# Blocks of 32 instead of 16 in a triangular inverse: the solve in three parts between other work, one join level fewer, units prepared a query group sooner

## The chip, the cores and the metric

The kernel runs on one core of a Trainium2 chip. The metric is the device time in microseconds of one execution. One program computes two networks, one behind the other: a first block (stages mix0, mlp0, mix1, mlp1; 512 tokens, model width 1024) and a second block of two layers (layer0, layer1; 16 meta tokens ahead of the 512, so 528). The change touches only the two layers of the second block, each in the same way.

## What is computed

Each layer of the second block adds a mixer and a gated feed-forward part. The mixer has two branches and gates on them: sparse attention (4 heads, keys chosen by an indexer) and a gated DeltaNet (4 heads of 128), whose chunks of tokens need the solution of a unit lower triangular system:

```python
m = jnp.where(strict, bc[..., None] * kk * decay, 0.0)
lhs = m + jnp.eye(CHUNK, dtype=f32)
rhs = jnp.concatenate([vc * bc[..., None], kc * (bc * jnp.exp(gcum))[..., None]], axis=-1)
sol = lax.linalg.triangular_solve(lhs, rhs, left_side=True, lower=True, unit_diagonal=True)
u, w = sol[..., :A_DV], sol[..., A_DV:]
...
v_new = u_c - jnp.einsum('bhcd,bhde->bhce', w_c, S)
o = (jnp.einsum('bhcd,bhde->bhce', q_c * jnp.exp(g_c)[..., None], S)
     + jnp.einsum('bhcs,bhse->bhce', qk_c, v_new))
S = (S * jnp.exp(g_last)[..., None, None]
     + jnp.einsum('bhcd,bhce->bhde', k_c * jnp.exp(g_last[..., None] - g_c)[..., None], v_new))
```

`S` goes from chunk to chunk, so the chunks run one behind the other. Everything is float32.

## The kernel before

**Weights.** All weights are streamed from HBM in 436 pieces of 128x1024. SyncE loads a piece, ScalarE rounds it to `w_hi` (L1314), GpSimd makes the remainder `w_lo` (L631, four instructions a piece), and TensorE multiplies in three passes (`n_hi,w_hi`, `n_lo,w_hi`, `n_hi,w_lo`).

**Filling.** In the attention and DeltaNet stages of a layer TensorE has a hand-set order. The small matmuls of the stage stand between pieces of projection work that depends on nothing in the stage, the fillers (the output gate `z`, the branch gates). `fill(blocks)` issues that many blocks of the current piece; a block is six matmuls (L1068), a piece is eight blocks. A piece adds up in one pair of PSUM banks, so the next piece waits until VectorE has evicted the last one (semaphore `taken`; evictions L2464, L2576). The tables `SCORE_FILL`, `VALUE_FILL` (attention) and `FILL` (the slots below) say how many blocks stand where.

**Attention.** `attention()` runs over four query groups j = 0 to 3 of 128 queries. A group first has its score phase: for each of four heads TensorE makes the scores (L1241, L1246), VectorE shifts them (L2848, L2851, with a row reduction), ScalarE exponentiates them (L1924), VectorE normalises them (L2862, L2863). VectorE takes a head's normalisation after the next head's shift. Then the value phase: transposes (L1272), copies on ScalarE (L1943), products with the values (L1280).

**Units.** The 528 tokens are five units: unit 0 with the 16 meta tokens, units 1 to 4 with 128 each. The matrices of a unit are prepared inside the attention (`prepare_keys` and `prepare_queries` on TensorE, `prepare` on VectorE with `unit_staged` as its output), and ScalarE sends them to an array `unit_scratch` in HBM. `NEXT_UNIT` and `EARLY` say in which query group.

**Inverse.** The inverse of `lhs` is built in two steps. The diagonal blocks of 16x16 of all units are read back from the scratch array, one block to a partition and two sets (128 partitions x 2 x 256 elements), and inverted on VectorE by substitution (`solve_blocks`): 15 steps of one multiplication (L2746) and one subtraction (L2749), then a transposing copy (L2750). `send_solved` writes the inverses X and their transposes Y back with ScalarE's DMAs, in rows of 64 bytes. Then the unit is read as whole 128x128 matrices of four heads (`fetch_unit`: M, X, Y). TensorE and VectorE join neighbouring blocks at the levels 4, 5 and 6, from 16 to 32, 64 and 128: `join_half` (4 matmuls), a copy on ScalarE (`p`, L1845), `join` (8 matmuls, or 4 at the last level, where only Y is needed), and subtractions on VectorE (L2795, L2796 by `joined_both`; L2838). Unit 0 has a single 16x16 block and needs no join.

**Slots.** Behind the attention come slots s = 0 to 5. Slot s joins unit s (s = 1 to 4), makes its `w` and `u` (`w_and_u`) and takes unit s - 1 through the recurrence (`step_v`, `step_state`, `step_out`). In `tokens` (L1104, L1105) keys and values are turned to rows of tokens; `v_tok` (L1860) are ScalarE's copies of the latter. In all loops the queue of each engine is in order, so an instruction that waits holds up all behind it on its engine.

## Time and profile before

| | |
|---|---|
| median of 3 runs | 2883.15 us (2881.82 to 2883.48) |
| the profiled execution | 2884.77 us |
| its span, first to last instruction | 2882.9 us |
| mean granted TensorE clock | 0.994 |
| TensorE busy | 2831.2 us, 98% of the span |
| VectorE, ScalarE, GpSimd busy | 51%, 35%, 48% |

The span lies in the profiled execution's time; 1.9 us of that lie around it. Layer 0 has its attention and slots from about 1300 to 1530 us of the span, layer 1 some 891 us later with the same pattern. A row of a timeline begins with start and duration in us; what stands in brackets at its end is how long the engine was idle before it, and who ended that. "ACTq" is ScalarE issuing a DMA. The clock is a share of 2.4 GHz.

### The profile page before, as it was taken

How to read it: one execution, taken by the hardware profiler on the slowest of the kernel's cores; microseconds unless marked ns; L12 is line 12 of the kernel's file. 1: busy time of each engine (PE TensorE's matmuls, PEld its weight loads, DVE VectorE, ACT ScalarE, POOL GpSimd, SP SyncE). 2: the span in 40 equal slices, each digit the busy share in tenths (PEclk: the TensorE clock that was granted, in tenths of full speed). 3: DMA queues.
4: the chain of work that ended last, by engine and by line, in shares of the span. 5: the costliest groups of instructions: out<-in, count | busy, mean ns of one | idle time of the engine just before them, and what ended most of it. 6: DMA issues, size and time to landing. Idle time of an engine off the chain costs nothing.

```text
span 2882.9 us, 43826 instructions
## 1 busy us (share of the span) xinstructions
PE 2831.2 (98%) x17572; PEld 2496.0 (87%) x17572; DVE 1463.4 (51%) x2401; ACT 1000.5 (35%) x1494; POOL 1374.4 (48%) x1748
## 2 busy tenths in 40 slices
PE   9999999999999999999999999999999999999999
PEld 7768888877788888998899999999988799999887
DVE  8955322267532227896445544234797545444241
ACT  4453222255322224433443322223443434322221
POOL 6416554555655455542125555456552214555554
PEclk9989999999999999999999999999999999999999
DMA  5103333322333334222414233223322423333322
GB/s 186 59 22 103 101 95 89 102 95 73 96 101 89 95 102 125 97 76 87 112 56 144 85 93 92 88 90 94 111 79 64 123 69 105 106 100 91 96 95 73
DMA packets 124622, 271.09 MB, mean 94 GB/s; under 512 B 22808, under 2 KB 59032, under 8 KB 124184
## 3 DMA queue, kind: packets, MB, share of 16 engines
q1 hardware_dynamic: 73104, 246.05, 27.1%
q10 hardware_dynamic: 51336, 22.41, 2.9%
q8 instruction: 139, 2.28, 0.3%
q14 instruction: 43, 0.35, 0.0%
HBM read 250.35 MB, written 18.07 MB: 93 GB/s over the span
## 4 chain that ended last, share of the span: by engine, by line
PE 86%; DVE 10%; issue 1%; ACT 1%; ACTq 1%; POOL 0%; DMA 0%; DVEq 0%; POOLq 0%
PE acc L659 65%; PE acc L1068 5%; PE aux L1082 3%; PE acc L708 3%; DVE index_score L2686 2%; PE acc L1049 2%; PE aux L1049 2%; DVE best L2682 2%; PE acc L692 1%; DVE conv_out L2101 1%; PE acc L1082 1%; PE aux L959 1%; PE acc L1280 1%; PE acc L782 1%; PE aux L846 0%
## 5 line engine op out<-in xcount | busy, mean ns | idle before, releaser
L631 POOL TENSOR_TENSOR w_lo<-w_raw,w_hi 128x256 fp32r<-128x256 f32 x1744 | 1374.2, 820 | 1492.3 <-ACT w_hi L1314 1491.6
L659 PE MATMUL acc<-n_hi,w_hi 128*128 128x264 f32 (+1 forms) x2824 | 757.1, 323 | 2.3 <-DVE index_k L2387 1.3
L659 PE MATMUL acc<-n_lo,w_hi 128*128 128x264 f32 (+1 forms) x2824 | 748.1, 320 | 0.0
L659 PE MATMUL acc<-n_hi,w_lo 128*128 128x264 f32 (+1 forms) x2824 | 746.0, 319 | 0.0
L1314 ACT ACTIVATE w_hi<-w_raw 128x1024 fp32r<-128x1024 f32 (+1 forms) x436 | 454.4, 1044 | 628.9 <-PE acc L659 560.9
L659 PEld LDWEIGHTS acc<-n_hi,w_hi 128*128 128x128 f32 x2824 | 470.4, 188 | 60.7 <-issue 15.9
L659 PEld LDWEIGHTS acc<-n_lo,w_hi 128*128 128x128 f32 x2824 | 467.2, 188 | 40.9 <-issue 2.6
L659 PEld LDWEIGHTS acc<-n_hi,w_lo 128*128 128x128 f32 x2824 | 467.2, 188 | 38.3
L2203 DVE TENSOR_TENSOR x<-x,acc 128x512 f32<-128x512 f32 (+1 forms) x144 | 99.7, 692 | 565.6 <-PE acc L659 519.2
L659 PE MATMUL acc<-hidden_lo,w_hi 128*128 128x512 f32 (+1 forms) x1040 | 343.3, 358 | 0.0
L659 PE MATMUL acc<-hidden_hi,w_lo 128*128 128x512 f32 (+1 forms) x1040 | 342.7, 357 | 0.0
L659 PE MATMUL acc<-hidden_hi,w_hi 128*128 128x512 f32 (+1 forms) x1040 | 342.7, 357 | 0.0
L659 PEld LDWEIGHTS acc<-hidden_lo,w_hi 128*128 128x128 f32 x1040 | 183.8, 188 | 31.0
L659 PEld LDWEIGHTS acc<-hidden_hi,w_hi 128*128 128x128 f32 x1040 | 183.5, 188 | 31.0
L659 PEld LDWEIGHTS acc<-hidden_hi,w_lo 128*128 128x128 f32 x1040 | 184.1, 188 | 30.0
L2364 DVE SCALAR_TENSOR_TENSOR unit_a<-acc,norm_scale 128x512 f32<-128x512 f32 x64 | 44.3, 692 | 196.3 <-PE acc L659 196.1
L1599 ACT ACTIVATE hidden_hi<-unit_b 128x512 fp32r<-128x512 f32 x64 | 40.5, 632 | 260.4 <-DVE unit_b L2369 260.4
L1068 PE MATMUL acc<-n_hi,w_hi 128*128 128x264 f32 x480 | 120.0, 332 | 6.4 <-DVE x L2464 2.7
L1770 ACT ACTIVATE squares<-unit_b 128x528 f32<-128x528 f32 x44 | 28.4, 646 | 261.8 <-DVE unit_b L2652 261.8
L2641 DVE TENSOR_TENSOR unit_a<-acc,norm_scale 128x528 f32<-128x528 f32 x44 | 31.1, 708 | 167.2 <-PE acc L659 167.1
L1068 PE MATMUL acc<-n_lo,w_hi 128*128 128x264 f32 x480 | 98.6, 287 | 0.0
L1068 PE MATMUL acc<-n_hi,w_lo 128*128 128x264 f32 x480 | 98.5, 287 | 0.0
(490 smaller groups left out, 3781.8 us busy)
## 6 DMA issues: line engine op xcount, KB each, us to landing
w_raw<-in_stream SPq DMA_DIRECT2D x420, 512.0 KB, 3.5
unit_blocks<-unit_scratch ACTq DMA_DIRECT2D x30, 256.0 KB, 4.9
w_raw<-in_stream SPq DMA_DIRECT2D x16, 384.0 KB, 3.0
unit_scratch<-unit_staged ACTq DMA_DIRECT2D x20, 256.0 KB, 2.6
saved_x<-x SPq DMA_DIRECT2D x2, 2112.0 KB, 9.4
x<-saved_x SPq DMA_DIRECT2D x16, 264.0 KB, 2.7
saved_gates<-root ACTq DMA_DIRECT2D x12, 264.0 KB, 2.1
unit_scratch<-unit_staged ACTq DMA_DIRECT2D x1, 2560.0 KB, 12.9
```

Of the source, the lines that this page charges most:

```text
L631: i = pool.tensor_tensor(wl[:, slot, s], raw[:, slot, s], wh[:, slot, s].bitcast(F32), ALU.subtract)
L659: last = pe.matmul(o, w[:, p % W_SLOTS, P * b:P * b + P], r, start=(b == 0 and i == 0), stop=(b == n - 1 and i == 2))
L708: mm = pe.matmul(acc[:, bank_of(p), :], w[:, p % W_SLOTS, P * b:P * b + P], v[b], start=(n == 0 and i == 0), stop=(n == KT - 1 and i == 2))
L1049: mm = pe.matmul(banks[:, 2 * g + s, 0:HALF], w[:, p % W_SLOTS, P * b:P * b + P], v[:, b, HALF * s:HALF * s + HALF], start=(b == 4 * g and ...
L1068: mm = pe.matmul(acc[:, s, 0:HALF], w[:, p % W_SLOTS, P * b:P * b + P], v[:, b, HALF * s:HALF * s + HALF], start=(b == 0 and i == 0), stop ...
L1082: return pe.matmul(out, lhs, rhs, start=start, stop=stop)
L1314: act.activation(wh[:, q % W_SLOTS, 0:n], raw[:, q % RAW_SLOTS, 0:n], ACT.Copy)\
L1599: act.activation(hid_hi[:, q % 2, m, ROW], sb_[:, m % 2, 0:SEQ], ACT.Copy)\
L2203: dve.tensor_tensor(xm, xm, a, ALU.add).then_inc(taken, c.made(taken))
L2364: dve.scalar_tensor_tensor(u, a, 0.0, scale[:, ROW], ALU.max, ALU.mult)\
L2682: latest[j] = step(dve.max(best[:, j - 1, :], s))
L2686: latest[j] = step(dve.match_replace(s, best[:, j - 1, :], s, MARK))
```

## The change

- **Blocks.** `SMALL` goes from 16 to 32, `LEVELS` from (4, 5, 6) to (5, 6). A joined unit has two `join_half` and two joins, of which the last is the short one. Gone for each joined unit are one `join_half` and one full join: 12 matmuls of 128x128, their ScalarE copy and two VectorE subtractions.
- **The solve.** 68 blocks (4 units x 4 heads x 4, and the 4 of unit 0) lie on 68 partitions, and the substitution has 31 steps, 62 instructions. Step j works on (31 - j)(j + 1) elements of a partition: 31 at both ends, 256 in the middle. It is in parts: the start and steps 0 to 9 behind the normalisation of query group 2; steps 10 to 15 inside the score phase of group 3, two behind the shift of each of the heads 0, 1, 2; steps 16 to 23 behind its last normalisation; then the eviction of the filler `z` 0; then steps 24 to 30, and the transposing copy of 1024 elements. Before, all stood ahead of that eviction.
- **The tiles.** `solved` and `turned` lie in the tiles `squares` and `unit_b`, which the slots use; so VectorE now waits for `solved_sent` before it clears `decayed` (in `squares`), and this stands ahead of the eviction of `z` 1.
- **Units** are prepared sooner: in group 0 unit 1, ahead of group 1 unit 2, in group 1 unit 3, ahead of group 2 unit 4. Groups 2 and 3 prepare none. The blocks are fetched after head 2 of group 2.
- **Sending.** Y of unit 0 is sent first, with a semaphore of its own; unit 0 waits for that alone and reads only its Y. The rows are 128 bytes long, 4224 of them where there were 4160 of 64.
- **Slots.** `FILL`: slot 0 gets 8 and 4 blocks ([8, 4]), slots 1 to 4 seven blocks each instead of eight (in slot 3 one of them directly ahead of `w_and_u`, in the others none). `step_out` goes ahead of the second `join_half`. On ScalarE the `v_tok` copies come first in slot 0, SiLU of `z` 0 and 1 moves to slot 1, five gate tiles move from slot 0 to slot 5, and `fetch_unit(u + 1)` stands behind the `v_tok` copies of slot u, where `fetch_unit(u + 2)` stood at the slot's end. On VectorE the last subtraction of a join comes ahead of `out_mean`.

The core of the diff; left out are declarations of tiles and semaphores, and places that follow from the tables:

```diff
@@ -60,10 +60,11 @@
-FILL = [[8, 0, 0, 0, 0, 0, 0]] + [[1, 1, 1, 2, 1, 1, 1]] * 4 + [[2, 1, 2, 0, 0, 0, 3]]
-SCORE_FILL = [[1, 2, 1, 0], [2, 2, 2, 2], [3, 2, 1, 0], [2, 2, 2, 2]]
-TAKEN_BEFORE = [3, 4, 3, 4]
-EARLY, NEXT_UNIT = {2: 3}, (1, 2, 4)
+FILL = [[8, 4, 0, 0, 0, 0, 0], [1, 1, 1, 1, 1, 2, 0], [1, 1, 1, 1, 1, 2, 0], [1, 1, 1, 1, 1, 1, 1], [1, 1, 1, 1, 1, 2, 0],
+        [2, 1, 2, 0, 0, 0, 3]]
+SCORE_FILL = [[1, 2, 1, 0], [3, 2, 1, 0], [3, 2, 1, 0], [2, 2, 2, 2]]
+TAKEN_BEFORE = [3, 3, 3, 4]
+EARLY, NEXT_UNIT = {1: 2, 2: 4}, {0: 1, 1: 3}
@@ -206,8 +207,12 @@
-SMALL = 16
-LEVELS = (4, 5, 6)
+SMALL = 32
+LEVELS = (5, 6)
+LAST = len(LEVELS) - 1
+SOLVED = 4 * A_HEADS * (P // SMALL)
+SOLVES = SOLVED + A_HEADS
+SOLVE_BEGIN, SOLVE_HEADS, SOLVE_BREAK = 10, 2, 24
@@ -1201,18 +1208,14 @@
+            if v >= 0:
+                step_out(v)
             if joined:
                 join_half(u, 1)
             fill(FILL[s][4])
             if joined:
                 join(u, 1)
-            if v >= 0:
-                step_out(v)
-            if joined:
-                join_half(u, 2)
             fill(FILL[s][5])
-            if joined:
-                join(u, 2)
@@ -1813,14 +1816,14 @@
-            act.dma_start(lt[0:A_HEADS, 1, :, :], small_blocks(M_PART, 0)).then_inc(blocks_landed, 16)
-            act.dma_start(lt[:, 0, :, :], small_blocks(M_PART, 1)).then_inc(blocks_landed, 16)
+            act.dma_start(lt[SOLVED:SOLVES, :, :], small_blocks(M_PART, 0)).then_inc(blocks_landed, 16)
+            act.dma_start(lt[0:SOLVED, :, :], small_blocks(M_PART, 1)).then_inc(blocks_landed, 16)
         def send_solved():
             act.wait_ge(blocks_solved, c.next(blocks_solved))
+            act.dma_start(small_blocks(Y_PART, 0), turned[SOLVED:SOLVES, :, :]).then_inc(first_sent, 16)
             for part, t in ((X_PART, solved), (Y_PART, turned)):
-                act.dma_start(small_blocks(part, 0), t[0:A_HEADS, 1, :, :]).then_inc(solved_sent, 16)
-                act.dma_start(small_blocks(part, 1), t[:, 0, :, :]).then_inc(solved_sent, 16)
+                act.dma_start(small_blocks(part, 1), t[0:SOLVED, :, :]).then_inc(solved_sent, 16)
@@ -1859,21 +1860,26 @@
+            if joined and u + 1 < UNITS:
+                fetch_unit(u + 1)
+            if u == UNITS:
+                for m in range(TOP_GATES - 1, KT):
+                    gate_tile(m, at["piece"] - 1)
             if u == 0:
-                silu_of_z(done[0, 0][1], z_piece)
-                for m in range(TOP_GATES - 1, KT):
-                    gate_tile(m, z_piece - 1)
-            gap(1)
+                job()
+            else:
+                gap(1)
             if joined:
                 half(acc[:, 2 + v % 2, :])
+            if u == 1:
+                silu_of_z(ATTN_FILLERS[7][1], at["piece"] - 1)
+                job()
+                silu_of_z(done[0, 0][1], at["piece"] - 1)
             gap(2)
             gap(3)
             if joined:
                 half(aux[:, 0, :])
             gap(4)
-            gap(5)
-            if joined:
-                half(aux[:, 0, :])
@@ -1898,8 +1905,6 @@
-                if u + 2 < UNITS:
-                    fetch_unit(u + 2)
@@ -1932,9 +1936,9 @@
-                    if j == 3 and h == 1:
+                    if j == 2 and h == 2:
                         fetch_blocks()
-                if j < 3:
+                if j in NEXT_UNIT:
@@ -1951,15 +1955,14 @@
-                if j < 2:
-                    send(j)
+                if j == 0:
+                    send(0)
                 if j < 3:
                     filler(*ATTN_FILLERS[2 * j + 1])
-            fetch_unit(0, (M_PART,))
-            act.wait_ge(solved_sent, c.next(solved_sent, 64))
-            fetch_unit(0, (X_PART, Y_PART))
+            act.wait_ge(first_sent, c.next(first_sent, 16))
+            fetch_unit(0, (Y_PART,))
             fetch_qk(0)
-            filler(*ATTN_FILLERS[7])
+            act.wait_ge(solved_sent, c.next(solved_sent, 32))
@@ -2570,13 +2573,12 @@
-                    if m == 5:
-                        dve.wait_ge(solved_sent, 64 * (l + 1))
             attention(l, filler)
+            dve.wait_ge(solved_sent, 32 * (l + 1))
@@ -2733,21 +2735,32 @@
-        def solve_blocks(l):
-            step(dve.memset(rt[:, 0:2 * SMALL * SMALL], 0.0))
+        def solve_start(l):
+            flat = solved[0:SOLVES].rearrange("p r c -> p (r c)")
+            step(dve.memset(flat, 0.0))
             dve.wait_ge(*c.mine())
-            dve.wait_ge(*step(dve.memset(rt[:, 0:2 * SMALL * SMALL].rearrange("p (s i) -> p s i", s=2)[:, :, ::SMALL + 1], 1.0)))
+            step(dve.memset(flat[:, ::SMALL + 1], 1.0))
             dve.wait_ge(blocks_landed, 32 * (l + 1))
-            for j in range(SMALL - 1):
+        def solve_rows(a, z):
+            for j in range(a, z):
                 n = SMALL - 1 - j
-                shape = [P, 2, n, j + 1]
-                rows, t = solved[:, :, j + 1:, 0:j + 1], products[:, :, 0:n, 0:j + 1]
+                shape = [SOLVES, n, j + 1]
+                rows = solved[0:SOLVES, j + 1:, 0:j + 1]
+                t = products[0:SOLVES, 0:n * (j + 1)].rearrange("p (n c) -> p n c", n=n)
+                dve.wait_ge(*c.mine())
                 dve.wait_ge(*step(dve.tensor_tensor(
-                    t, lt[:, :, j, j + 1:].rearrange("p s (n o) -> p s n o", o=1).to_broadcast(shape),
-                    solved[:, :, j:j + 1, 0:j + 1].to_broadcast(shape), ALU.mult)))
-                dve.wait_ge(*step(dve.tensor_tensor(rows, rows, t, ALU.subtract)))
-            dve.tensor_copy(turned, solved.rearrange("p s r c -> p s c r")).then_inc(blocks_solved, c.made(blocks_solved))
+                    t, lt[0:SOLVES, j, j + 1:].rearrange("p (n o) -> p n o", o=1).to_broadcast(shape),
+                    solved[0:SOLVES, j:j + 1, 0:j + 1].to_broadcast(shape), ALU.mult)))
+                step(dve.tensor_tensor(rows, rows, t, ALU.subtract))
+        def solve_end(l):
+            dve.wait_ge(*c.mine())
+            dve.wait_ge(bo_full, 5 * (l + 1))
+            dve.tensor_copy(turned[0:SOLVES], solved[0:SOLVES].rearrange("p r c -> p c r"))\
+                .then_inc(blocks_solved, c.made(blocks_solved))
@@ -2818,24 +2831,20 @@
-                join_block(2)
             gap(2)
+            if s >= 2:
+                copy_out(s - 2)
             if joined:
                 written = joined_both()
-            if s >= 2:
-                copy_out(s - 2)
             gap(3)
             gap(4)
-            if joined:
-                dve.wait_ge(*written)
-                written = joined_both()
-            gap(5)
-            if v >= 0:
-                out_mean(v)
             if joined:
                 dve.wait_ge(uy_full, c.next(uy_full))
                 dve.wait_ge(*written)
                 dve.tensor_tensor(y_in, y_in, by_head(aux[:, 2, :]), ALU.subtract).then_inc(uy_ready, c.made(uy_ready))
+            if v >= 0:
+                out_mean(v)
+            gap(5)
@@ -2889,18 +2897,25 @@
+                    if j == 3 and h < 3:
+                        solve_rows(SOLVE_BEGIN + SOLVE_HEADS * h, SOLVE_BEGIN + SOLVE_HEADS * (h + 1))
                 if TAKEN_BEFORE[j] == B_HEADS:
                     filler(*ATTN_FILLERS[2 * j])
                 normalise(j, B_HEADS - 1)
+                if j in NEXT_UNIT:
+                    prepare(NEXT_UNIT[j], l)
+                if j == 2:
+                    solve_start(l)
+                    solve_rows(0, SOLVE_BEGIN)
                 if j < 3:
-                    prepare(NEXT_UNIT[j], l)
                     filler(*ATTN_FILLERS[2 * j + 1])
                 if j + 1 in EARLY:
                     prepare(EARLY[j + 1], l)
             c.next(bt_full, 5)
-            dve.wait_ge(gate_sent, c.at(gate_sent))
-            solve_blocks(l)
+            solve_rows(SOLVE_BEGIN + 3 * SOLVE_HEADS, SOLVE_BREAK)
             filler(*ATTN_FILLERS[7])
+            solve_rows(SOLVE_BREAK, SMALL - 1)
+            solve_end(l)
```

TensorE's queue in slot 1 of layer 0, before. `join_half(1)` is the product of `unit_blocks` and `unit_a`, then the join of its level with `p`, then `step_out` (`v_new,qk_t`), then `join_half(2)` with `unit_b`:

```order
L1082 MATMUL aux<-unit_blocks,unit_a 128x128 [waits join_ready,join_block_ready]
L1082 MATMUL aux<-unit_blocks,unit_a 128x128 x3
L1068 MATMUL acc<-n_hi,w_hi 128x264 x2
L1068 MATMUL acc<-n_lo,w_hi 128x264 x2
L1068 MATMUL acc<-n_hi,w_lo 128x264 x2
L1082 MATMUL aux<-p_117,unit_blocks 128x128 [waits join_half_ready]
L1082 MATMUL aux<-p_117,unit_blocks 128x128 x3
L1082 MATMUL aux<-unit_blocks,p_117 128x128 x4
L1082 MATMUL aux<-v_new,qk_t 16x128 [waits qk_t_landed_0]
L1082 MATMUL aux<-v_new,qk_t 16x128 x3
L1082 MATMUL aux<-unit_blocks,unit_b 128x128 [waits join_ready,join_block_ready]
L1082 MATMUL aux<-unit_blocks,unit_b 128x128 x3
```

And the same slot in the changed kernel, from the fill behind its first full join on:

```order
L1075 MATMUL acc<-n_hi,w_hi 128x264 x2
L1075 MATMUL acc<-n_lo,w_hi 128x264 x2
L1075 MATMUL acc<-n_hi,w_lo 128x264 x2
L1089 MATMUL aux<-v_new,qk_t 16x128 [waits qk_t_landed_0]
L1089 MATMUL aux<-v_new,qk_t 16x128 x3
L1089 MATMUL aux<-unit_blocks,unit_a 128x128 [waits join_ready,join_block_ready]
L1089 MATMUL aux<-unit_blocks,unit_a 128x128 x3
L1075 MATMUL acc<-n_hi,w_hi 128x264 [waits acc_taken,w_lo_ready]
L1075 MATMUL acc<-n_hi,w_hi 128x264
L1075 MATMUL acc<-n_lo,w_hi 128x264 x2
L1075 MATMUL acc<-n_hi,w_lo 128x264 x2
L1089 MATMUL aux<-unit_blocks,p_118 128x128 [waits join_half_ready]
```

`step_out` stands ahead of the last `join_half`, the level in between is gone, and a fill takes its place.

VectorE's queue in the score phase of query group 3, from the first head's shift to the second head's normalisation, before:

```order
L2851 ISA probs,row_values_110<-aux,select_bias 128x528 [waits dsa_scores_full,dsa_turned]
L2851 ISA row_values_110 128x1
L2855 TENSOR_SCALAR row_values_110<-row_values_110,scales_by_token 128x1 [waits dve_steps]
L2851 ISA probs,row_values_110<-aux,select_bias 128x528 [waits dsa_scores_full]
L2851 ISA row_values_110 128x1
L2855 TENSOR_SCALAR row_values_110<-row_values_110,scales_by_token 128x1 [waits dve_steps]
L2862 RECIPROCAL row_values_110<-row_values_110 128x1 [waits dsa_exp]
L2863 TENSOR_SCALAR probs<-probs,row_values_110 128x528 [waits dve_steps]
```

And now:

```order
L2860 ISA probs,row_values_110<-aux,select_bias 128x528 [waits dsa_scores_full,dsa_turned]
L2860 ISA row_values_110 128x1
L2864 TENSOR_SCALAR row_values_110<-row_values_110,scales_by_token 128x1 [waits dve_steps]
L2754 TENSOR_TENSOR solve_products<-solve_blocks,squares 68x231 [waits dsa_shifted]
L2757 TENSOR_TENSOR squares<-squares,solve_products 68x21x11 [waits dve_steps]
L2754 TENSOR_TENSOR solve_products<-solve_blocks,squares 68x240 [waits dve_steps]
L2757 TENSOR_TENSOR squares<-squares,solve_products 68x20x12 [waits dve_steps]
L2860 ISA probs,row_values_110<-aux,select_bias 128x528 [waits dsa_scores_full]
L2860 ISA row_values_110 128x1
L2864 TENSOR_SCALAR row_values_110<-row_values_110,scales_by_token 128x1 [waits dve_steps]
L2871 RECIPROCAL row_values_110<-row_values_110 128x1 [waits dsa_exp]
L2872 TENSOR_SCALAR probs<-probs,row_values_110 128x528 [waits dve_steps]
```

Four instructions of the solve stand between two heads' shifts.

VectorE's queue at the end of the solve and the start of slot 0, before. `delta_z` is the eviction of a `z` filler, the MEMSET clears `decayed`:

```order
L2749 TENSOR_TENSOR root<-root,attn_v 128x2x15 [waits dve_steps]
L2750 COPY unit_a<-root 128x512 [waits dve_steps]
L2576 TENSOR_TENSOR delta_z<-acc,norm_scale 128x528 [waits w_piece_used]
L2580 MEMSET squares 128x512
L2576 TENSOR_TENSOR delta_z<-acc,norm_scale 128x528 [waits w_piece_used]
L2807 TENSOR_TENSOR k_g_in<-aux,gates_by_token 128x512 [waits tokens_full]
```

And now:

```order
L2754 TENSOR_TENSOR solve_products<-solve_blocks,squares 68x31 [waits dve_steps]
L2757 TENSOR_TENSOR squares<-squares,solve_products 68x31 [waits dve_steps]
L2762 COPY unit_b<-squares 68x1024 [waits dsa_out_full,dve_steps]
L2582 MEMSET squares 128x512 [waits solved_sent]
L2577 TENSOR_TENSOR delta_z<-acc,norm_scale 128x528 [waits w_piece_used]
L2820 TENSOR_TENSOR k_g_in<-aux,gates_by_token 128x512 [waits tokens_full]
```

The eviction of `z` 0 is ahead of the last seven steps (not shown), the copy stands behind it, and MEMSET and the second eviction stand behind the wait for `solved_sent`.

## Rows read from the trace of the kernel before

**Rows 1.** The page, busy time of TensorE (us, share of the span, instructions).
```profile
PE 2831.2 (98%) x17572; PEld 2496.0 (87%) x17572; DVE 1463.4 (51%) x2401; ACT 1000.5 (35%) x1494; POOL 1374.4 (48%) x1748
```

**Rows 2.** Waits of TensorE: waiter, releaser; sum us, times, longest us.
```profile
PE aux L1082 <- ACT v_new L1849: 2.0, 6, 0.5
...
PE aux L1082 <- DVE unit_blocks L2796: 1.1, 2, 0.6
```

**Rows 3.** Timeline of TensorE, one joined unit: start us, duration us, instruction.
```profile
1442.64 1.13 PE L1082 MATMUL aux<-unit_blocks,unit_a 128*128 128x128 f32 x8
...
1443.52 0.49 PE L1068 MATMUL acc<-n_hi,w_hi 128*128 128x264 f32 x2
...
1444.45 1.16 PE L1082 MATMUL aux<-p,unit_blocks 128*128 128x128 f32 x8
...
1446.34 0.39 PE L1082 MATMUL aux<-squares,delta_q 128*128 128x128 f32 x2
```

**Rows 4.** Timeline of TensorE, places where it waited, and blocks behind them.
```profile
1303.54 1.54 PE L1082 MATMUL acc<-delta_k 128*128 128x128 f32 x8 [2.44 <-DVE x L2464]
...
1385.10 0.48 PE L1068 MATMUL acc<-n_hi,w_hi 128*128 128x264 f32 x2 [0.91 <-DVE x L2464]
...
1408.93 1.13 PE L1138 MATMUL acc<-v_tok,unit_blocks 128*128 128x128 f32 x8 [2.72 <-ACT v_tok L1860]
...
1409.81 0.65 PE L1068 MATMUL acc<-n_hi,w_hi 128*128 128x264 f32 x2
...
1411.14 1.05 PE L1104 MATMUL aux<-const,delta_k 128*128 128x128 f32 x4
```

**Rows 5.** Windows: busy us of the engines, then PEclk, DMA share, GB/s.
```profile
1408.00:1412.00 4.00, 3.07 (x19) 3.10 (x20) 0.69 (x1) 3.97 (x9) 2.66 (x4) 0.75 1.04 285
...
1412.00:1416.00 4.00, 3.54 (x25) 3.33 (x25) 1.65 (x3) 3.41 (x9) 0.00 (x0) 0.83 0.98 291
```

**Rows 6.** Timeline of TensorE in query groups 1 and 2.
```profile
1328.27 0.48 PE L1068 MATMUL acc<-n_hi,w_hi 128*128 128x264 f32 x2 [0.43 <-DVE x L2464]
...
1360.00 1.05 PE L1082 MATMUL aux<-const,gates_by_token 128*128 128x128 f32 x8
...
1363.24 1.03 PE L1272 MATMUL aux<-const,probs 128*16 128x128 f32 x8
```

**Rows 7.** Timeline of VectorE, query groups 2 and 3, and the solve.
```profile
1360.09 0.70 DVE L2576 TENSOR_TENSOR root<-acc,norm_scale 128x528 f32<-128x528 f32 x1
...
1362.61 0.43 DVE L2863 TENSOR_SCALAR probs<-probs,row_values 128x400 f32<-128x400 f32 x1
...
1380.42 0.71 DVE L2851 CUSTOM_DVE_ANT_0 probs<-aux,select_bias 128x528 f32<-128x528 f32 x1 [0.78 <-PE aux L1246]
...
1384.25 0.70 DVE L2464 TENSOR_TENSOR x<-acc,norm_scale 128x528 f32<-128x528 f32 x1
...
1386.56 0.65 DVE L2749 TENSOR_TENSOR root<-root,attn_v 128x30 f32<-128x30 f32 x1
...
1391.66 0.29 DVE L2746 TENSOR_TENSOR attn_v<-index_k,root 128x128 f32<-128x128 f32 x1
...
1395.87 0.19 DVE L2746 TENSOR_TENSOR attn_v<-index_k,root 128x30 f32<-128x30 f32 x1
...
1398.40 0.71 DVE L2576 TENSOR_TENSOR delta_z<-acc,norm_scale 128x528 f32<-128x528 f32 x1 [1.47 <-PE acc L1068]
```

**Rows 8.** Timeline of GpSimd at the start of query group 3.
```profile
1375.50 2.82 POOL L631 TENSOR_TENSOR w_lo<-w_raw,w_hi 128x256 fp32r<-128x256 f32 x4 [8.38 <-ACT w_hi L1314]
```

**Rows 9.** Timeline of ScalarE's DMA issues behind the solve.
```profile
1396.96 0.28 ACTq L1822 DMA_DIRECT2D unit_scratch<-root  x1
...
1399.00 4.18 ACTq L1827 DMA_DIRECT2D unit_blocks<-unit_scratch  x3
```

**Rows 10.** DMA packets in 1399:1401 (64 B) and in 1414:1416 (512 B).
```profile
DMA packets 2686, 0.17 MB, mean 85 GB/s; under 512 B 2686, under 2 KB 2686, under 8 KB 2686
...
DMA packets 1162, 0.66 MB, mean 329 GB/s; under 512 B 32, under 2 KB 1140, under 8 KB 1162
```

35 lines of the change are left out of this document (17 added, 18 removed).

## The prediction

> **What bounds the kernel now.** I read the page first: TensorE is busy for 98% of the span [rows 1], so only what TensorE need not do, or where it waits, moves the time. Then its waits by releaser, for the small stalls around the joins [rows 2]; then TensorE's timeline through one slot, for the price of a join [rows 3], and at its long stalls, for what follows them [rows 4]; last VectorE's timeline through query groups 2 and 3, since the changed solve goes into VectorE's idle time there [rows 7]. Times are those of layer 0; layer 1 repeats the pattern, so each sum is taken twice. The sum is made against the profiled execution's 2884.77 us and carried over to the median of 2883.15 us, 1.6 us below it.
>
> **What is removed.** A `join_half` runs from 1442.64 to 1443.52, 0.88 us; a full join from 1444.45 to 1446.34, 1.89 us [rows 3]. In the slots TensorE changes between fills and joins, and at each change some 0.15 us are lost: between 1443.52 and 1444.45 lie a fill of one block (0.74 us at full speed, three pairs of matmuls) and 0.19 us more. With three such changes gone, 0.45 us, a joined unit saves 0.88 + 1.89 + 0.45 = 3.2 us, four units 12.9 us. TensorE's wait for the second subtraction in slot 1, 0.56 us (1.1 us in the two layers), goes with the join, since the fills of a slot then lie between fewer hand-overs, and of the waits for `v_new` up to 0.5 us each I take one, 0.35 us [rows 2]. Together **-13.8 us** a layer. The ScalarE copy and the VectorE subtractions of that level save nothing of their own.
>
> **What the tables move.** Blocks of fill are the same in number, so they cost nothing in themselves. (a) Slot 1: ScalarE has two SiLU and their table load ahead of the copy that the last join needs; I take +0.2. (b) Slot 3: its piece ends at the sixth place, and the block ahead of `w_and_u` starts the next, so it waits for the eviction behind VectorE's subtraction. The stall at 1385.10 has the same shape, a fill behind an eviction, and was 0.91 us [rows 4]: +0.9. (c) Query group 2: one unit's keys leave it for group 1. They ran from 1360.00 for 1.7 us (two products of eight matmuls), beside the eviction of 1360.09 to 1360.79 [rows 6, 7]; now the next fill waits there for that eviction, 0.85 us. The value phase began at 1363.24, right behind the last normalisation (1362.61 + 0.43) [rows 6, 7], and can't begin sooner. So the 1.7 us are paid in group 1 and not won in group 2; the 0.43 us of wait at 1328.27 [rows 6] goes, by the new places of the fills. +1.3. The queries cost as much in one group as in the other. (d) Steps 0 to 9 are 20 instructions, 6.7 us by the price below. From some 1366.4, when I expect the blocks, they end at 1373.1, and the eviction of group 3's first filler is wanted at 1373.4. VectorE is free there, and I count 0; there is no cover beyond 0.3 us, and each us that the blocks land later is a us more.
>
> **The price of a step.** One instruction over 30 elements took 0.19 us, over 128 elements 0.29 us [rows 7]: 0.16 us and 1.04 ns per element, and 0.03 us between two. No row shows 256 elements with a broadcast over 68 partitions. The bounds are 0.29 us (cost flat above 128) and twice the slope, 0.69 us; I take the line, 0.42 us, since it held between 30 and 128. The row at 1386.56 took 0.65 us for 30 elements, when GpSimd worked on a `w_lo`; such instructions lie in GpSimd's bursts of 4, one of which ran from 1375.50 to 1378.32 [rows 7, 8].
>
> **The steps inside the score phase.** VectorE is idle 0.78 us ahead of each shift [rows 7]; a head's two steps need 4 x (0.41 + 0.03) = 1.8 us. The first four lie in the burst: 4 x (0.65 + 0.03) = 2.7 us from 1376.5 to 1379.25, where the second shift began 1.2 us sooner. Each of the next two heads adds 1.8 - 0.78 = 1.0 us. So VectorE is 3.3 us late at the last head, and the eviction of 1384.25 comes at 1387.6. TensorE's next fill waits for it (0.91 us before [rows 4]): **+3.3**. Now the clock. The waits of 2.44 and 2.72 us were followed by slow matmuls: eight in 1.54 us instead of 1.13 to 1.16, and a block of fill in 1.33 us (1409.81 to 1411.14) instead of 0.74; that is the 1.2 GHz level. After the 0.91 us the matmuls ran at full speed, 0.48 us for the first pair [rows 3, 4]. Behind the 2.72 us the granted clock was 0.75 and 0.83 in two windows of 4 us: 1.0 + 0.7 = 1.7 us lost [rows 5]. The late eviction gives two stalls of about 1.0 us at the heads and one of some 2.2 us. That is nearer to 2.44 than to 0.91, so I count the same loss: **+1.7**.
>
> **The end of the solve and slot 0.** Call the start of the eviction of `z` 0 E; before it was 1398.40 [rows 7]. The solve used to be done 1.5 us ahead of it. Now behind the eviction (0.75) come steps 24 to 30, 14 instructions over 756 elements twice: 14 x 0.19 + 1512 x 1.04 ns = 4.2 us, and the copy of 1024 elements, 1.2 us. So the blocks are solved at E + 6.2. Sending took from 1396.96 to about 1402.1 (three fetch issues end at 1403.18, two of them, some 0.55 us each, behind the wait) [rows 9]: 5.1 us. The packets are 128 bytes instead of 64. In 2 us went 2686 of 64 or 1162 of 512 bytes, which is 11.9 and 27.5 ns a packet on each of 16 engines [rows 10]; between them 128 bytes cost 14.1 ns, and 4224 packets 3.7 us against 3.1 for 4160: +0.6. `solved_sent` is there at E + 11.9, clearing and the eviction of `z` 1 take 1.0 more, and the four blocks start at E + 12.9. TensorE has had eight blocks and `tokens` until E + 9.4, after 1.6 us of idleness, because ScalarE copies the attention's output behind the three issues. So it stands still for 3.5 us, but for one product, and the clock is low behind that: four blocks at 1.33 us, slot 1 starts at E + 18.2. Before, it started at 1409.81 = E + 11.4 [rows 4], paid 1.7 to 1.8 us of low clock behind it, and had 2.9 us of fill that now lie in slot 0. 18.2 - 11.4 - 1.8 - 2.9 = **+2.1**.
>
> The Trainium skill ("DMA: Bandwidth & Descriptors", "Why small descriptors are slow (HBM only)") has a fixed overhead of about three cycles a packet over beats of 32 bytes, by which 128 bytes cost 7 cycles where 64 cost 5. By that estimate the 3.1 us of transfer become 4.4, and slot 1 would be 0.7 us later in each layer than in the sum above. The rows' 11.9 and 27.5 ns grow less from 64 to 512 bytes than the page's 5 to 19 cycles, so the trace speaks for the smaller sum.
>
> **Sum.** -13.8 + 0.2 + 0.9 + 1.3 + 3.3 + 1.7 + 2.1 = -4.3 us a layer, -8.6 in both: 2876.2 us for a profiled execution like the one before, **2874.5 us** for the median. Its own range is 2870 to 2879.
>
> **The rivals.**
> - *The covers hold (chance 0.23).* VectorE's steps cost the flat 0.29 us above 128 elements and GpSimd's burst falls elsewhere. Then a head has 1.3 us of steps in 0.78 us of gap, the last head is 1.6 us late instead of 3.3, and no stall is long enough for the clock: 1.7 + 1.7 less, and slot 0 0.6 less. 4.0 x 2 = 8 us under the forecast: 2866.5. For it: VectorE is busy half the time only [rows 1]. Against it: the line from 30 to 128 elements.
> - *Nothing of the solve is on the path (0.07).* The joins alone: -13.8 + 0.2 + 0.9 = -12.7 a layer, 2857.7 us. Against it: 3.5 us of standstill in slot 0 by any price of a step, since the sending alone took 5.1 us.
> - *The blocks land late (0.18).* The fetch now comes in group 2, right behind the sending of the last units. Landing 1 to 4 us after 1366.4, the steps 0 to 9 push the eviction ahead of group 3 by as much: 2877 to 2882 us, a gain within the uncertainty for the most part. For it: no cover beyond 0.3 us. Against it: units are prepared a group sooner.
> - *Slower (0.12): VectorE's products with a broadcast cost twice per element.* Steps 0 to 9 then end 2.6 us late, the heads take 4 x 0.25 = 1.0 us more each, 3.0, and the last steps and the copy 2.6 more: +8.2 a layer, 2874.5 + 16.4 = 2891 us. It decides when VectorE's excess is over 4.3 us a layer; at over 7.2 it is measurably slower. For it: more of the solve is exposed than before, when it lay wholly in the value phase. Against it: the 128-element instructions of before have the same operands, with the same broadcast, and follow the line.
> - The change does what it says: the order of the instructions shows twelve matmuls fewer per joined unit, so I give that rival nothing.
>
> **The numbers.** The forecast has 0.40. A measurement of this kernel can tell about 0.2%, 5.8 us: faster means under 2877.4, slower above 2888.9. Faster: 0.23 + 0.07 + most of the forecast's 0.40 (its upper end passes 2877.4), 0.36, = 0.66. Same: 0.04 + 0.18 = 0.22. Slower 0.12. The range leaves out the second rival (0.07) and the slower one (0.12): 2860 to 2883 us; the bounds of a step's price lie in it on the lower side, and on the upper side with the slower rival beyond it.
>
> **What the new profile would show.** Slots 1 to 4 some 3.2 us shorter each; a gap of 1.0 us ahead of the third and fourth heads' fills and some 2 us ahead of the first fill of group 3's value phase; VectorE's steps of 0.40 to 0.43 us at 240 to 256 elements; a granted clock below 0.8 behind that stall; the MEMSET of `squares` 11.9 us behind the eviction of `z` 0; five gate tiles in slot 5 without a wait of TensorE. I am wrong if the stalls at the heads are absent (faster), if the first step waits for `blocks_landed` beyond 1367, or if slot 5's tiles hold up the output.

## The result, and the profile after

The changed kernel takes 2869.59 us (median of 5 runs, 2865.16 to 2870.63), the kernel before 2882.45 us in the same comparison (5 runs). The ratio is 0.9948, with a 95% interval of 0.9937 to 0.9960: faster by 12.9 us. The forecast was 2874.5 us, 8.6 us faster. The direction and the range (2860 to 2883) hold; the median lies 0.4 us under the likeliest case's own range (2870 to 2879). The profiled execution went from 2884.77 to 2869.59 us, its span from 2882.9 to 2867.7 us, 15.2 us; the one of before stood 2.3 us above its median.

The page of the changed kernel, span and busy times, against [rows 1]:

```profile
span 2867.7 us, 43456 instructions
...
PE 2806.9 (98%) x17380; PEld 2476.1 (86%) x17380; DVE 1478.1 (52%) x2439; ACT 998.6 (35%) x1488; POOL 1377.0 (48%) x1748
```

TensorE has 192 entries fewer (the 96 removed matmuls have two each) and 24 us less work; the span fell by 15. So TensorE is idle some 9 us longer than before, all in all. Where they are is seen in TensorE's timeline, layer 0, from the score phase of query group 3 to slot 1:

```profile
1374.85 1.05 PE L1249 MATMUL aux<-attn_k,attn_q 128*128 128x264 f32 x4
...
1380.70 1.16 PE L1249 MATMUL aux<-attn_k,attn_q 128*128 128x264 f32 x4 [0.76 <-DVE row_values L2864]
...
1383.98 1.16 PE L1249 MATMUL aux<-attn_k,attn_q 128*128 128x264 f32 x4 [0.66 <-DVE row_values L2864]
...
1388.58 0.48 PE L1075 MATMUL acc<-n_hi,w_hi 128*128 128x264 f32 x2 [1.99 <-DVE x L2467]
...
1404.11 0.48 PE L1075 MATMUL acc<-n_hi,w_hi 128*128 128x264 f32 x2 [0.89 <-DVE delta_z L2577]
...
1412.20 0.66 PE L1111 MATMUL aux<-const,delta_k 128*128 128x128 f32 x4 [2.01 <-ACT attn_out L1955]
...
1416.17 0.78 PE L1075 MATMUL acc<-n_hi,w_hi 128*128 128x264 f32 x2 [2.62 <-DVE delta_z L2577]
...
1420.76 1.05 PE L1145 MATMUL acc<-v_tok,unit_blocks 128*128 128x128 f32 x8
...
1434.62 1.05 PE L1145 MATMUL acc<-v_tok,unit_blocks 128*128 128x128 f32 x8
```

The three waits for VectorE at the heads are 0.76, 0.66 and 1.99 us where there was one of 0.91 [rows 4]. Slot 0 has waits of 2.01 and 2.62 us where there was one of 2.72. Windows of 4 us behind the long waits (busy times, then the granted clock):

```profile
1384.00:1388.00 4.00, 2.60 (x16) 2.25 (x16) 3.76 (x11) 1.62 (x4) 0.00 (x0) 1.00 0.00 0
1388.00:1392.00 4.00, 3.42 (x17) 3.14 (x18) 3.83 (x7) 1.13 (x3) 2.80 (x4) 0.63 0.02 4
...
1412.00:1416.00 4.00, 1.35 (x8) 0.95 (x8) 1.02 (x3) 0.14 (x1) 0.00 (x0) 0.61 0.95 200
1416.00:1420.00 4.00, 3.83 (x18) 3.86 (x19) 1.22 (x3) 2.09 (x5) 0.91 (x2) 0.53 0.95 261
1420.00:1424.00 4.00, 4.00 (x37) 4.00 (x36) 1.24 (x2) 1.14 (x4) 1.88 (x3) 1.00 0.27 74
```

The clock was below 1.0 in both places, and full in between (1396 to 1412). VectorE's timeline shows the solve, in its three parts, and what stood behind it:

```profile
1366.71 0.30 DVE L2754 TENSOR_TENSOR solve_products<-solve_blocks,squares 68x31 f32<-68x31 f32 x1 [0.94 <-DMA solve_blocks<-unit_scratch]
...
1373.55 0.38 DVE L2757 TENSOR_TENSOR squares<-squares,solve_products 68x220 f32<-68x220 f32 x1
1375.05 0.71 DVE L2467 TENSOR_TENSOR x<-acc,norm_scale 128x528 f32<-128x528 f32 x1 [1.12 <-PE acc L1075]
...
1378.51 0.83 DVE L2754 TENSOR_TENSOR solve_products<-solve_blocks,squares 68x240 f32<-68x240 f32 x1
...
1385.93 0.42 DVE L2757 TENSOR_TENSOR squares<-squares,solve_products 68x256 f32<-68x256 f32 x1
...
1387.74 0.70 DVE L2467 TENSOR_TENSOR x<-acc,norm_scale 128x528 f32<-128x528 f32 x1
...
1397.21 0.36 DVE L2757 TENSOR_TENSOR squares<-squares,solve_products 68x192 f32<-68x192 f32 x1
1403.26 0.71 DVE L2577 TENSOR_TENSOR delta_z<-acc,norm_scale 128x528 f32<-128x528 f32 x1 [5.69 <-PE acc L1075]
...
1408.23 1.12 DVE L2762 COPY unit_b<-squares 68x1024 f32<-68x1024 f32 x1
1414.97 0.48 DVE L2582 MEMSET squares<- 128x512 f32 x1 [5.63 <-DMA unit_scratch<-unit_b]
...
1422.15 0.69 DVE L2803 TENSOR_TENSOR unit_a<-unit_blocks,const 128x512 f32<-128x512 f32 x1 [4.93 <-DMA unit_blocks<-unit_scratch]
```

An instruction over 256 elements took 0.42 us, as the line of [rows 7] gave. In the second part VectorE never rests; ahead of the eviction of `z` 0 it is idle for 5.69 us. The chain behind the copy is long: solved at 1409.35, `solved_sent` at 1414.97, unit 1 landed at 1422.15.

Between the same events in both traces (after minus before, us):

| stretch | layer 0 | layer 1 | forecast |
|---|---|---|---|
| keys of group 0 to first scores of group 3 | +0.83 | +1.25 | +1.3 |
| to the first fill behind group 3's scores | +3.03 | +3.04 | +3.3 |
| to the first fill behind `z` 0's eviction | +1.38 | +1.28 | +1.7 |
| to the product of `v_tok` in slot 0 | +6.97 | +7.38 | +6.8 |
| from there to the same product in slot 4 | -20.29 | -20.17 | -17.4 |
| to the first block of the output projection | +0.29 | +0.27 | 0 |

In the fifth row 2.9 us are the four blocks of fill that went to slot 0. The forecast of that row is the sum of its terms: -13.8 + 0.2 + 0.9, less 2.9 for the blocks and 1.8 for the low clock that slot 1 used to have. The rows add up to -7.8 and -7.0 us where the forecast had -4.3; of these 6.1 us between the two, 5.7 are in slots 1 to 4.

### The profile page after: what moved, and what is told of

The parts are those of the page before. It is cut to its first block, busy times and chain, and to the rows that moved or that the text cites. A ratio compares the mean times of both kernels' runs of the same rounds, so it can differ in the third digit from the quotient of the medians.

```text
span 2867.7 us, 43456 instructions
## 1 busy us (share of the span) xinstructions
PE 2806.9 (98%) x17380; PEld 2476.1 (86%) x17380; DVE 1478.1 (52%) x2439; ACT 998.6 (35%) x1488; POOL 1377.0 (48%) x1748
## 4 chain that ended last, share of the span: by engine, by line
PE 87%; DVE 10%; issue 2%; ACT 1%; DMA 0%; POOL 0%; ACTq 0%; DVEq 0%; POOLq 0%
PE acc L666 65%; PE acc L1075 5%; PE acc L715 3%; PE aux L1089 3%; DVE index_score L2688 2%; PE acc L1056 2%; PE aux L1056 2%; DVE best L2684 2%; PE acc L699 1%; PE acc L1283 1%; DVE conv_out L2104 1%; PE aux L966 1%; PE acc L1089 1%; PE acc L789 1%; PE aux L853 0%
## 5 line engine op out<-in xcount | busy, mean ns | idle before, releaser
L666 PEld LDWEIGHTS acc<-n_hi,w_hi 128*128 128x128 f32 x2824 | 470.4, 188 | 60.7 <-issue 15.9
L1075 PEld LDWEIGHTS acc<-n_hi,w_hi 128*128 128x128 f32 x480 | 79.3, 197 | 35.8 <-issue 33.1
```

The lines of the kernel that those rows point to most:

```text
L666: last = pe.matmul(o, w[:, p % W_SLOTS, P * b:P * b + P], r, start=(b == 0 and i == 0), stop=(b == n - 1 and i == 2))
L1075: mm = pe.matmul(acc[:, s, 0:HALF], w[:, p % W_SLOTS, P * b:P * b + P], v[:, b, HALF * s:HALF * s + HALF], start=(b == 0 and i == 0), stop ...
```

## The experiments

Each ratio is to the kernel before, timed again beside the run. Those medians lie between 2882.7 and 2884.7 us, and in the traces the keys of group 0 in layer 0, ahead of which no edit changes anything, start anywhere from 1301.0 to 1305.3 us. So a difference of 2 us between the times of two runs says little. The stretches between two events of the slots repeat within 0.1 us from run to run where no edit touches them, and the readings below rest on them.

### Where slots 1 to 4 got shorter

**The level alone.** The kernel before, without the join of the level 5. This run and the two that build on it leave out one of the joins, so they do not compute the whole inverse; they serve for the time alone. The parts of ScalarE and VectorE that go with it are left out below.

```diff
-LEVELS = (4, 5, 6)
+LEVELS = (4, 6)
...
-            if joined:
-                join_half(u, 1)
             fill(FILL[s][4])
-            if joined:
-                join(u, 1)
             if v >= 0:
                 step_out(v)
             if joined:
-                join_half(u, 2)
+                join_half(u, 1)
             fill(FILL[s][5])
             if joined:
-                join(u, 2)
+                join(u, 1)
```

> The kernel before, with the join of the level 5 left out (one join_half, one full join, the ScalarE copy and the two subtractions of each joined unit); nothing else is changed, so the output is not the reference's: its neighbours 32 apart are not joined. The changed kernel gained 2.6 us a layer more in slots 1 to 4 than my sum had. Theory A: a joined unit saves 3.2 us of TensorE's own time plus the waits of slot 1, as in the sum, and the excess came with the new order inside the slots (two blocks ahead of w_and_u, step_out sooner, fetches sooner). Then slots 1 to 4 of layer 0, 84.65 us before, take 84.65 - 13.8 = 70.9 us here, and the time is 2882.5 - 27.6 = 2855 us. Theory B: the removal itself carries all of it, because the waits for v_new and for the last subtraction go with the hand-overs of that level. Then the slots take 84.65 - 16.4 = 68.3 us and the time is 2849.5 us.

Measured: 2858.68 us, ratio 0.9914 (0.9900 to 0.9927) to before. TensorE's timeline of it, the product of `v_tok` in slots 0 and 4, and below it its waits for `v_new`:

```profile
1409.52 1.35 PE L1138 MATMUL acc<-v_tok,unit_blocks 128*128 128x128 f32 x8 [2.72 <-ACT v_tok L1856]
...
1482.27 1.16 PE L1138 MATMUL acc<-v_tok,unit_blocks 128*128 128x128 f32 x8
```

```profile
PE aux L1082 <- ACT v_new L1845: 2.1, 6, 0.5
```

Between them lie 72.75 us where there were 85.53: 12.8 us less, so theory B is out. The four slots became shorter by 3.7, 3.0, 3.0 and 3.0 us. Slot 1 has the additional 0.7 because TensorE's wait of 0.56 us for the second subtraction [rows 2] went with the level. So a join is worth 3.0 us, not the 3.2 of the forecast. The six waits for `v_new` are as before [rows 2], and the wait for the last subtraction of a join is there too. It stands among the waits of the weight load, where the kernel before has it as well; first before, then here:

```profile
PEld acc L1138 <- DVE unit_blocks L2838: 2.0, 8, 0.3
```

```profile
PEld acc L1138 <- DVE unit_blocks L2828: 2.1, 8, 0.3
```

**The order in the slots.** The same, and the changed kernel's order within a slot; below is TensorE's part. On VectorE the last subtraction comes ahead of `out_mean`, and `copy_out` ahead of `joined_both`.

```diff
-FILL = [[8, 0, 0, 0, 0, 0, 0]] + [[1, 1, 1, 2, 1, 1, 1]] * 4 + [[2, 1, 2, 0, 0, 0, 3]]
+FILL = [[8, 0, 0, 0, 0, 0, 0]] + [[1, 1, 1, 1, 1, 3, 0]] * 4 + [[2, 1, 2, 0, 0, 0, 3]]
...
             fill(FILL[s][3])
-            fill(FILL[s][4])
             if v >= 0:
                 step_out(v)
             if joined:
                 join_half(u, 1)
-            fill(FILL[s][5])
+            fill(FILL[s][4])
             if joined:
                 join(u, 1)
+            fill(FILL[s][5])
```

> The kernel before without the join of the level 5 (as in the run on the joins alone; the output is not the reference's for the same reason), and now also with the changed kernel's order inside the slots: step_out ahead of the last join_half and one block sooner, fills [1, 1, 1, 1, 1, 3, 0], the last subtraction ahead of out_mean, copy_out ahead of joined_both. With the level alone left out slots 1 to 4 of layer 0 took 72.75 us and the kernel 2858.7 us, and the six waits for v_new were all still there. Theory A (the excess of 2.7 us a layer over my sum is the order's: an earlier step_out moves the squares, the root and its table load on ScalarE out of the way of v_new): the waits for v_new are gone, slots 1 to 4 take about 70.0 us, 2853.3 us. Theory B (it came with the sooner fetches or with seven blocks a slot instead of eight): the slots stay within 1 us of 72.75 and the time within 2 us of 2858.7.

Measured: 2854.94 us, ratio 0.9900 (0.9884 to 0.9917); the stretch is 71.37 us (1406.42 to 1477.79), 1.4 us less. TensorE's waits for `v_new`:

```profile
PE aux L1082 <- ACT v_new L1845: 2.1, 6, 0.5
```

My mechanism was wrong, and the stretch lies between the two theories. The waits for `v_new` are all still there, so an earlier `step_out` did nothing for them. Gone from the weight load's waits is the row of the last subtraction, some 0.26 us a slot, since three blocks now stand between the last join and `w_and_u` where one stood. That is 1.0 of the 1.4 us; I have no separate measurement for the rest. The changed kernel has two blocks at that place in each of the slots 1 to 4, and not only one in slot 3 as my description of the change has it, and the row is gone there too.

**The place of the fetches.** The same, and `fetch_unit` of the next unit behind the `v_tok` copies.

```diff
                         .then_inc(vb_ready, c.made(vb_ready))
+            if joined and u + 1 < UNITS:
+                fetch_unit(u + 1)
...
-                if u + 2 < UNITS:
-                    fetch_unit(u + 2)
```

> The kernel before without the join of the level 5 and with the changed order in the slots (the last run of that kind, 71.37 us for slots 1 to 4 of layer 0, 2854.9 us; its six waits for v_new, 2.1 us, are still there, so the sooner step_out had not removed them), and now also with fetch_unit of the next unit behind the v_tok copies instead of at the slot's end. The output is not the reference's, as there. Theory A (ScalarE issued three DMAs, 1.6 us, between w and the root, and so came late to v_new): the waits for v_new are gone, slots 1 to 4 take 70.3 us, 2852.7 us. Theory B (the table load for the root makes v_new late, wherever the fetches stand): the waits stay, 71.4 us, 2854.9 us.

Measured: 2851.26 us, ratio 0.9888 (0.9873 to 0.9903); the stretch is 69.41 us (1409.40 to 1478.81), 2.0 us less again, a little more than theory A had. TensorE's waits of the kind went from six to two:

```profile
PE aux L1082 <- ACT v_new L1845: 0.9, 2, 0.4
```

Why is seen on ScalarE at the end of slot 1, first in the run before this one:

```profile
1425.40 0.60 ACT L1891 ACTIVATE w_t<-aux 128x512 f32<-128x512 f32 x1 [3.30 <-PE aux L1082]
1425.40 1.48 ACTq L1823 DMA_DIRECT2D unit_blocks<-unit_scratch  x3
1427.21 1.28 ACT L1881 ACT_TABLE_LOAD   x1 [1.21 <-issue]
1428.51 0.30 ACT L1881 ACTIVATE row_values<-row_values,eps 16x4 f32<-16x4 f32 x1
1428.71 0.57 ACT L1845 ACTIVATE v_new<-acc 128x512 f32<-128x512 f32 x1
```

and then here:

```profile
1428.37 0.60 ACT L1893 ACTIVATE w_t<-aux 128x512 f32<-128x512 f32 x1 [3.30 <-PE aux L1082]
1428.98 1.28 ACT L1883 ACT_TABLE_LOAD   x1
...
1430.48 0.57 ACT L1845 ACTIVATE v_new<-acc 128x512 f32<-128x512 f32 x1
```

Three DMA issues, 1.48 us together, stood between `w_t` and the table load, and `v_new` began 3.31 us behind `w_t` instead of 2.11: 1.2 us late. Issuing a DMA is no busy time of ScalarE, so the page shows nothing of it; "[1.21 <-issue]" does. The gain is all in slots 2 and 3 (1.1 and 0.9 us). TensorE's waits for `v_new` were 0.52 and 0.23 us of it; behind each stood a shorter one of the weight load, 0.25 and 0.28 us, for the join block `unit_a`, which VectorE makes behind the same root of ScalarE. Both are gone.

**What the changed kernel has besides.** It keeps none of the waits for `v_new`, while the last run still has one in slot 1. ScalarE and TensorE there, first in the last run:

```profile
1411.14 3.24 ACT L1604 ACTIVATE x<-x,vec 128x528 f32<-128x528 f32 x5
...
1414.29 0.57 ACT L1845 ACTIVATE v_new<-acc 128x512 f32<-128x512 f32 x1
...
1414.91 1.16 PE L1082 MATMUL aux<-v_new,k_g_out 128*128 128x128 f32 x8 [0.45 <-ACT v_new L1845]
```

and in the changed kernel:

```profile
1421.85 0.60 ACT L1852 ACTIVATE v_new<-acc 128x512 f32<-128x512 f32 x1 [2.84 <-PE acc L1145]
...
1423.99 1.05 PE L1089 MATMUL aux<-v_new,k_g_out 128*128 128x128 f32 x8
```

Five gate tiles (3.24 us) stood ahead of `v_new`, and the changed kernel has moved them to slot 5. From the last pair of the fill to the product are 0.25 us instead of 0.85: 0.6 us won. No run moved the tiles alone, so this is a reading of two traces and not a test.

With that the stretch is accounted for: 85.53 - 12.8 (the level) - 1.4 (the order) - 2.0 (the fetches) = 69.4 us, less 0.6 (the gate tiles), 1.7 (the low clock behind slot 0, which the changed kernel lacks here) and 2.9 (the four moved blocks), and 1.0 more for the new wait of 0.96 us in slot 3, make 65.2 us. Measured are 65.24. Slot by slot 0.1 us stay open in slot 1, and 0.2 in slot 3, with the opposite sign.

### What the parts of the solve cost

**No steps in the score phase.**

```diff
-SOLVE_BEGIN, SOLVE_HEADS, SOLVE_BREAK = 10, 2, 24
+SOLVE_BEGIN, SOLVE_HEADS, SOLVE_BREAK = 10, 0, 24
```

> The changed kernel with steps 10 to 15 of the solve behind the last normalisation of query group 3 instead of two in each head (SOLVE_HEADS = 0). Theory A (the stall at the heads is VectorE's, and the low clock behind it follows from the stall): the first fill behind group 3's scores comes 3.0 us sooner, its wait falls from 1.99 to about 0.9 us, no window there shows a clock below 1.0, which is another 1.3 us; VectorE had 5.7 us of idle time ahead of z 0's eviction, the six steps need 5.3 us, so that eviction is late by 0.4 us at most. 3.9 us a layer, 2861.8 us. Theory B (the steps only move the wait): VectorE is late for z 0's eviction by as much as it was at the heads, slot 0 starts at the same time, and the time is within 2 us of 2869.6 us.

Measured: 2863.17 us, ratio 0.9930 (0.9916 to 0.9944), 6.4 us under the changed kernel. TensorE's timeline:

```profile
1385.88 0.48 PE L1075 MATMUL acc<-n_hi,w_hi 128*128 128x264 f32 x2 [0.90 <-DVE x L2467]
...
1400.98 0.48 PE L1075 MATMUL acc<-n_hi,w_hi 128*128 128x264 f32 x2 [1.85 <-DVE delta_z L2577]
```

From the keys of group 0 (1303.50) to the first of these fills are 82.38 us, 3.0 less than in the changed kernel (1303.16 to 1388.58), as theory A had it. But VectorE is late for `z` 0 by 1.85 - 0.89 = 0.96 us, not 0.4, so 3.5 us a layer are won and not 3.9. The windows around it (1384 to 1408) have a clock of 1.00.

**All steps ahead of the eviction of `z` 0.**

```diff
-SOLVE_BEGIN, SOLVE_HEADS, SOLVE_BREAK = 10, 2, 24
+SOLVE_BEGIN, SOLVE_HEADS, SOLVE_BREAK = 10, 2, 31
```

> The changed kernel with all steps of the solve ahead of z 0's eviction, the transposing copy alone behind it (SOLVE_BREAK = 31). VectorE was idle 5.7 us ahead of that eviction, steps 24 to 30 take 4.2 us. Theory A (the chain from the solve's end over the sending to the clearing, the eviction of z 1 and unit 1's landing bounds slot 0): the blocks are solved 4.2 us sooner, the wait of 2.0 us for attn_out is gone, that for z 1 falls from 2.6 to about 1 us, the clock stays high, and slot 1 starts 6.0 us sooner in each layer: 2857.6 us. Theory B (slot 0 is held by TensorE's twelve blocks and ScalarE's copies, the sending is hidden): slot 1 starts at most 1 us sooner, 2868 us.

Measured: 2856.89 us, ratio 0.9906 (0.9891 to 0.9921), 12.7 us under the changed kernel. Slot 0 on TensorE:

```profile
1403.67 0.48 PE L1075 MATMUL acc<-n_hi,w_hi 128*128 128x264 f32 x2 [0.89 <-DVE delta_z L2577]
...
1409.59 0.60 PE L1111 MATMUL aux<-const,delta_k 128*128 128x128 f32 x4
...
1411.96 0.48 PE L1075 MATMUL acc<-n_hi,w_hi 128*128 128x264 f32 x2 [1.34 <-DVE delta_z L2577]
...
1414.97 1.05 PE L1145 MATMUL acc<-v_tok,unit_blocks 128*128 128x128 f32 x8
```

`tokens` don't wait, the four blocks wait 1.34 us, and the first of them takes 0.48 us for its first pair, not 0.78: the clock stayed. From `z` 0's fill to the product are 11.3 us instead of 16.65. The seven steps filled a hole in VectorE that was there anyway.

### What stood behind what in slot 0

**The attention's output first.** ScalarE's copy ahead of `send_solved()`, alone.

```diff
-                if j == 3:
-                    send_solved()
                 act.wait_ge(bo_full, c.next(bo_full))
                 act.activation(ob[:, :, META + P * j:META + P * j + P],
                                acc[:, 2, :].rearrange("p (h q) -> p h q", h=4), ACT.Copy)\
                     .then_inc(bo_ready, c.made(bo_ready))
+                if j == 3:
+                    send_solved()
```

> The changed kernel with the copy of the attention's output ahead of the sending on ScalarE, alone. TensorE's wait for attn_out in slot 0, 2.01 and 2.68 us, is then gone. Theory A (the wait for z 1's eviction, behind solved_sent, stands behind it and takes all of it over): tokens start 2 us sooner, the wait ahead of the four blocks grows from 2.6 to 4.6 us, and the time stays at 2869.6 us within 1.5 us. Theory B (each wait costs by itself): 2 x 2.3 us less, 2865 us.

Measured: 2868.07 us, ratio 0.9947 (0.9933 to 0.9960). That is 1.5 us under the changed kernel, within theory A's margin. The wait for `attn_out` is gone, and the next one took it over whole:

```profile
1414.34 0.78 PE L1075 MATMUL acc<-n_hi,w_hi 128*128 128x264 f32 x2 [5.07 <-DVE delta_z L2577]
```

**The eviction of `z` 1 first.** VectorE's wait for `solved_sent` and the clearing behind it.

```diff
             attention(l, filler)
-            dve.wait_ge(solved_sent, 32 * (l + 1))
-            step(dve.memset(decayed, 0.0))
...
                     .then_inc(utok_ready, c.made(utok_ready))
+            if u == 0:
+                dve.wait_ge(solved_sent, 32 * (l + 1))
+                dve.wait_ge(*step(dve.memset(decayed, 0.0)))
             gap(1)
```

> The changed kernel with the wait for solved_sent and the clearing of decayed behind the eviction of z 1 and the scaling of unit 0's keys on VectorE, instead of ahead of them. The four blocks of slot 0 then wait for nothing but tokens, and start at about 1413.4 instead of 1416.2. Theory A (that order cost the stall): slot 1 starts 2.5 us sooner, 2864.6 us. Theory B (something stands behind it: unit 1's blocks landed at 1422.15, and the first join_half of slot 1 waits for them): slot 1 starts 2.5 us sooner and a new wait of TensorE for the join block, about 0.5 to 2.5 us, takes its place: 2865.6 to 2869.6 us.

Measured: 2864.84 us, ratio 0.9935 (0.9921 to 0.9948), 4.8 us under the changed kernel. The time is theory A's, but it did not come about as A had it. The four blocks no longer wait, and a new wait stands behind them, not the one that B named:

```profile
1420.14 1.13 PE L1145 MATMUL acc<-v_tok,unit_blocks 128*128 128x128 f32 x8 [1.70 <-ACT v_tok L1861]
```

ScalarE too has the wait for `solved_sent` and four DMA issues ahead of its `v_tok` copies. From `z` 0's fill to this product are 15.35 us instead of 16.65, and 14.33 instead of 17.05 in layer 1: 4.0 us in both. The rest is luck. At the heads TensorE has the same three waits as in the changed kernel (0.76, 0.67 and 1.98 us), and this time the clock did not fall behind them. The last of the waits, and the windows around and behind it:

```profile
1390.63 0.48 PE L1075 MATMUL acc<-n_hi,w_hi 128*128 128x264 f32 x2 [1.98 <-DVE x L2467]
```

```profile
1388.00:1392.00 4.00, 2.02 (x17) 1.84 (x16) 3.82 (x11) 1.87 (x3) 0.75 (x1) 1.00 0.02 4
1392.00:1396.00 4.00, 3.76 (x25) 2.69 (x24) 3.79 (x7) 1.06 (x2) 2.73 (x4) 1.00 0.10 19
```

From this fill to that of `z` 0 are 14.16 us, in layer 1 too, where the changed kernel needs 15.53 and 15.43. These 2.6 us lie ahead of the place that the edit touches. On the other hand layer 0 began 2.1 us later in this execution, ahead of all edits.

**Steps spread otherwise.**

```diff
-SOLVE_BEGIN, SOLVE_HEADS, SOLVE_BREAK = 10, 2, 24
+SOLVE_BEGIN, SOLVE_HEADS, SOLVE_BREAK = 11, 1, 28
```

> The changed kernel with steps 0 to 10 in query group 2, one step instead of two in each of the heads 0 to 2, and steps 28 to 30 behind z 0's eviction (SOLVE_BEGIN 11, SOLVE_HEADS 1, SOLVE_BREAK 28). Theory A (VectorE's work between group 3's first shift and the end of the solve is one chain with a fixed length; where it is put only moves the stall, but short stalls leave the clock high): the heads' stall falls by 1.9 us and the clock loss of 1.3 us goes; z 0's eviction is then late by 1.2 us; the blocks are solved 4.8 us sooner than in the changed kernel, slot 1 starts 5.0 to 6.6 us sooner: 2857 to 2860 us, not below the run with all steps ahead of the eviction (2856.9). Theory B (the stall at the heads costs apart from slot 0, so that both gains add): 2851 us.

Measured: 2855.19 us, ratio 0.9901 (0.9885 to 0.9918): between the theories. The fills behind the scores and behind `z` 0 waited 0.96 and 1.03 us, so one step in a head is hidden, and VectorE was hardly late for `z` 0, where I had counted 1.2 us. In slot 0 a wait of 2.11 us for `z` 1 was left in layer 0, with a granted clock of 0.62 in the window behind it (1408 to 1412), and one of 2.53 us in layer 1.

**With the three reorderings.** Steps 11, 1, 28, the two edits above, and the `v_tok` copies of unit 0 ahead of ScalarE's wait:

```diff
-            act.wait_ge(solved_sent, c.next(solved_sent, 32))
-            fetch_unit(1)
-            fetch_qk(1)
...
                         .then_inc(vb_ready, c.made(vb_ready))
+            if u == 0:
+                act.wait_ge(solved_sent, c.next(solved_sent, 32))
+                fetch_unit(1)
+                fetch_qk(1)
```

> The run before this one (steps 11, 1, 28), and further: the copy of the attention's output ahead of the sending, the eviction of z 1 ahead of the wait for solved_sent, the v_tok copies of unit 0 ahead of the same wait on ScalarE. TensorE's waits for attn_out and z 1 in slot 0 are then gone. Theory A (behind them stands the chain from the solve's end to unit 1's landing, 12.8 us, and the first join_half of slot 1 waits for it): a wait of some 2 us for the join block appears in slot 1, and the time is 2856 us. Theory B (unit 1 comes in time): slot 1 starts 2 us sooner still, 2852 us.

Measured: 2848.63 us, ratio 0.9881 (0.9864 to 0.9897). The wait for the join block that theory A named is there, shorter:

```profile
1413.40 1.16 PE L1089 MATMUL acc<-unit_blocks,unit_a 128*128 128x128 f32 x8 [1.05 <-DVE unit_a L2802]
```

In layer 1 it is 0.53 us. A's mechanism holds, but the wait was two to four times smaller than forecast, and the time lies 3.4 us under B and 7.4 us under A. Neither theory speaks of the low clock that the wait of 2.11 us had behind it: with that wait gone, every window from 1380 to 1424 has 1.00.

**The reorderings on all steps ahead of `z` 0.**

> All steps of the solve ahead of z 0's eviction (steps 10, 2, 31), with the three reorderings of the run before this one. The wait for z 1, 1.34 us in the run with SOLVE_BREAK = 31 alone, is gone; unit 1 lands 14.7 us behind the eviction of z 0, so that the first join_half of slot 1 is late by about 0.6 us. Theory A: 0.9 us a layer under that run's 2856.9, 2855 us. Theory B (nothing is late for unit 1): 2854 us or less, with no wait for the join block. Theory C (the reorderings cost elsewhere, the sending being later by the copy): 2857 us or more.

Measured: 2854.90 us, ratio 0.9897 (0.9881 to 0.9914), 2.0 us under the run with `SOLVE_BREAK` = 31 alone, and no wait in slot 0 or for the join block. The size is A's, the absent wait B's; the two forecasts lay 1 us apart, which these times do not resolve. What this run still pays is the stall at the heads (0.76, 0.67, 1.98 us) with its low clock (0.57 in 1388 to 1392); the run before it, with one step a head, doesn't.

**The fastest.** On that one: M of unit 1 fetched ahead of the wait, and other fills in slots 2 to 4.

```diff
-FILL = [[8, 4, 0, 0, 0, 0, 0], [1, 1, 1, 1, 1, 2, 0], [1, 1, 1, 1, 1, 2, 0], [1, 1, 1, 1, 1, 1, 1], [1, 1, 1, 1, 1, 2, 0],
+FILL = [[8, 4, 0, 0, 0, 0, 0], [1, 1, 1, 1, 1, 2, 0], [1, 1, 1, 1, 1, 2, 1], [1, 1, 1, 1, 1, 2, 0], [1, 1, 1, 1, 1, 1, 0],
...
             fetch_unit(0, (Y_PART,))
             fetch_qk(0)
+            fetch_unit(1, (M_PART,))
...
-                fetch_unit(1)
+                fetch_unit(1, (X_PART, Y_PART))
```

> The fastest kernel so far (2848.6 us: steps 11, 1, 28, and the three reorderings in slot 0), with M of unit 1 fetched ahead of the wait for solved_sent, and with the fills of slots 2 to 4 as [1, 1, 1, 1, 1, 2, 1], [1, 1, 1, 1, 1, 2, 0], [1, 1, 1, 1, 1, 1, 0], so that no piece ends right ahead of a fill. Theory A: the wait of 0.96 us for the eviction in slot 3 is gone, unit 1 lands about 0.7 us sooner, as two parts instead of three follow the solve, and the wait for the join block (1.05 and 0.53 us) shrinks by as much: 1.4 us a layer, 2845.8 us. Theory B (the landing of unit 1 is set by the 64-block writes and not by the number of parts fetched; the eviction's wait moves to the next fill): 2848 to 2849 us.

Measured: 2845.76 us, ratio 0.9868 (0.9853 to 0.9883), as theory A had it: 38 us under the kernel before, 24 us under the changed one. Neither the wait in slot 3 nor the one for the join block is left. The two edits were not run apart.

## Why the prediction was right, and where not

**The removed joins** came out close to their price: 13.8 us a layer forecast with the two small waits, 12.8 us measured with the level alone. It is 3.0 us a join and not 3.2, so 12.1 and not 12.9 us, and 0.7 for the wait for the second subtraction. The wait for `v_new`, 0.35 us of the sum, did not go with the level.

**The step that fell short** is a term that I left out. I wrote "Blocks of fill are the same in number, so they cost nothing in themselves" and booked the new order of the slots with losses alone (+0.2 and +0.9). The order gave 1.4 us a layer, most of it because more blocks cover the last subtraction, and the new place of the fetches 2.0 us, because three DMA issues no longer stand ahead of the root and `v_new` on ScalarE. Both were in rows of before: the waits for `v_new`, of which I took a third [rows 2], and a row of waits of the weight load that I didn't read. The third gain, by the traces, is the move of the gate tiles out of slot 0, 0.6 us. The +0.2 for SiLU in slot 1 was nothing: from the second `join_half` to the join are 1.84 us there, and 1.85 in the last of the three runs above, which has no SiLU there. Against these 4.0 us stands 1.0 us that the joins gave less than forecast. So part of the distance to the forecast cancelled, and the total hit better than its terms.

**The eviction in slot 3** was forecast at +0.9 and is 0.96 us; with the other fills of the last run it is gone.

**Query groups 1 and 2**: +1.3 forecast, +0.83 and +1.25 measured. The blocks landed at 1366.71 (1366.4 forecast). Steps 0 to 9 ended at 1373.93, 0.8 us later than forecast, since they began later and one instruction over 31 elements took 0.68 us beside a burst of GpSimd. It cost nothing, because the eviction was wanted at 1375.05 and not at 1373.4: VectorE still waited 1.12 us for it. So "no cover beyond 0.3 us" was wrong in my prediction: the cover was larger, and with it a first part of the lateness in the rival of late blocks was free.

**The heads**: +3.3 forecast, +3.03 measured, by the mechanism named: four instructions between two shifts, VectorE late and the eviction late with it. Taking the steps out of the heads gave back these 3.0 us, which shows it. Of the first four, which I had at 0.65 us each, the durations were 0.58, 0.81, 0.83 and 0.41 us: the sum of 2.7 us is right, the price of each is not, and that they meet is luck. The low clock behind the stall, +1.7, was +1.38 and +1.28. It is absent in the runs with one step or none in a head, whose windows at 1384 and 1388 have a clock of 1.00, so it needs the stall. But the stall alone doesn't bring it: in the run with the eviction of `z` 1 first the same three waits left the clock at 1.00 in both layers. I had tied the loss to the length of the wait; what else it takes, no run here shows. That it came in both layers of the changed kernel is in part luck.

**Slot 0**, with the forecast in brackets and E as in the prediction: the blocks solved at E + 6.1 (6.2), `solved_sent` 5.6 us later (5.7), the four blocks at E + 12.9 (12.9), the first fill of slot 1 at E + 18.3 (18.2). `SOLVE_BREAK` = 31 shows the chain to be the cause. The two waits in it don't add: taking away the first alone left the whole to the second. One premise was wrong without effect: the kernel before sends 4224 rows too, not 4160, which changes the sum by 0.05 us.

**The gate tiles**: in slot 5 TensorE waits 1.27 instead of 0.89 us ahead of the output projection, 0.3 us in the stretch, where I had 0; that the tiles are the cause was not tried.

Against the slower rival: an instruction over 256 elements with a broadcast took 0.42 us, not 0.69. Against the rival that nothing is on the path: the three stretches of new stalls cost 11.4 us in layer 0, of which only 2.9 are moved blocks, and the run that took them away without touching the other fills (2848.63 us) is 21 us faster than the changed kernel.

For the send, the Trainium skill's rule ("DMA: Bandwidth & Descriptors", "Why small descriptors are slow (HBM only)") had made it 6.4 us by the estimate in the prediction, where the sum by the rows had 5.7. Layer 0 took 5.6 us from the end of the copy to the MEMSET, layer 1 6.2 us, so this trace does not tell the two apart. In the five kernels in which VectorE waits there right behind the copy, the ten sends took 5.4 to 6.2 us, 5.8 in the mean, which is nearer to the rows.

## What to carry to other kernels

When work leaves the bound engine, look also at what else the edit reorders: waits of half a microsecond and less, and the DMA issues ahead of a small operation on an engine that works in order, gave back a quarter as much as the removed joins (3.4 of 12.8 us). When a run's time meets a forecast, check that it changed where the edit did: the run with the eviction of `z` 1 first met its forecast with 2.6 us from a place that the edit does not touch. A wait shown in front of an instruction is worth nothing alone if the next wait hangs on the same late event; look for the event (here the end of the solve) and move that. And put side work into the largest hole of its engine: the seven last steps stood behind a hole of 5.7 us that would have held them.

## What the runs showed of the hardware that I had not expected

- An operation of VectorE on two SBUF operands takes 0.4 us longer beside GpSimd's `w_lo`: 0.81 to 0.84 us instead of 0.40 to 0.42 over 231 to 255 elements, 0.65 instead of 0.19 to 0.22 over 30 [rows 7]. At full overlap the surcharge does not grow with the size. The Trainium skill ("SBUF — State Buffer", "Terms") says that the port pair which the two share is held for a whole instruction, and a constant surcharge agrees with that. GpSimd's four instructions took 3.13 and 3.48 us beside these operations, and 2.82 before [rows 8].
- Nearly the same waits of TensorE can leave its clock high or low. It stayed at 1.00 behind a wait of 1.85 us (no steps in the heads, 1400 to 1404). Behind waits of 0.76, 0.66 and 1.99 us within 8 us it fell to 0.63 (the changed kernel, 1388 to 1392), and behind 0.76, 0.67 and 1.98 us it stayed at 1.00 in both layers (the eviction of `z` 1 first, 1388 to 1396). A mean of 0.63 is a mixture of the two levels of 2.4 and 1.2 GHz: pairs of matmuls of a fill took 0.41 and 0.64 us. What decides, the runs don't show; so a loss of clock behind a stall of this size, 1.3 us here, is a chance and not a fixed price.
